# First attention, branch a: scores stacked over 128 rows instead of 64, with their operands split into roundings and remainders

## The chip, the core and the metric

The kernel is one program on one core of a Trainium2 chip. The metric is device time in microseconds (us); three runs of the kernel before gave 1660.15, 1660.17 and 1661.46 us, with a median of 1660.17 us.

The core's engines are named as in the profile: PE is TensorE (PEld its weight loads), DVE is VectorE, ACT is ScalarE, POOL is GpSimd, SP is SyncE, which here only issues transfers. All matrix products write to PSUM, eight banks of 128x512 fp32.

## What is computed

Two blocks run one after the other over 512 tokens of width 1024. Only the first attention of the first block is touched. In the reference it reads (shortened):

```python
def first_block(x, norm_gain, w_in, b_merge, rel_bias, ...):
    xn = rms_norm(x, norm_gain[0])
    qa, ka, va, ga, qb, kb, vb, gb, iq, ik, iw, za, zb = jnp.split(xn @ w_in[0], offsets, axis=-1)
    ya = chunked_relpos_attention(qa, ka, va, rel_bias[0]) * jax.nn.silu(ga)   # branch a, 8 heads of 64
    ...
    yb = dsa_sparse_attention(qb, kb, vb, iq, ik, iw) * jax.nn.silu(gb)        # branch b
    ...

def one_chunk(c):                                # inside chunked_relpos_attention
    s = jnp.einsum('bqhd,bkhd->bhqk', qc, kc).astype(jnp.float32) * scale + bias[None]
    s = jnp.where(valid[None, None], s, NEG)
    p = jax.nn.softmax(s, axis=-1).astype(v.dtype)
    return jnp.einsum('bhqk,bkhd->bqhd', p, vc)
```

All of it has to have fp32 accuracy.

## The kernel before

**Weights as slabs.** All weights come from DRAM as a stream of slabs of 128x1024 fp32 (512 KB) into RAW, a ring of four. For each slab `n`, ACT writes a rounded copy to WH (`high`, L1360, type fp32r) and POOL writes the remainder RAW - WH to WL (`low`, L671). A product in fp32 accuracy is then three fp32r products: WH with the rounded and with the remaining part of the input (L782, L783), and WL with the rounded part (L784). WH and WL hold two slabs, so ACT may round slab n only when slab n-2 has been used up, and POOL's remainder must be there before PE starts on slab n. Most jobs (`qa0`, `ga2` and so on) have one slab each and one PSUM bank, which ACT or DVE empties. In the order of the stream the jobs here are vbiw, iq0, iq1, ikb, qa0 to qa3, ka0 to ka3, va (four slabs), qb0 to qb3, ga0 to ga3, gb0 to gb3, za0 to za7. PE works through them in that order, with the indexer's products between qa1 and va.

**Queues.** Each engine runs its instructions in the order in which they are written; it waits at a semaphore (`wait_ge`) with all that stands behind it. Transfers are issued by SP (the slabs) and, in between its own work, by ACT. `split_past(name)` on ACT does the roundings of all slabs up to two behind the job's last one; `evac` calls it, waits for the job's products and empties its bank.

**The first attention** (`attention(segments["ab"])` on PE, ACT and DVE) goes over 32 pairs: first branch a, then branch b, each with four head pairs p and in each four blocks i of 128 queries. One pair is two heads e = 0, 1 against P * (i + 1) keys. In step k PE makes the scores of pair k (L919), two k-tiles of the jobs za and zb beside them (L782 to L784), the value products of pairs k-4 and k-3 (L894, in every second step) and the transposes of the probabilities of pair k-2 (L941). DVE adds the bias and takes the maximum (L2048) and later normalises (L2026, L2030); ACT takes the exponentials (L1455) and copies the transposed tile (L1466).

In branch a a head's scores are one product of 64 rows in full fp32: heads e = 0 and 1 lie in the lower and the upper 64 partitions of QA and KA. In branch b they are two fp32r products over 128 rows:

```python
yield dict(qk=[(QA[r, p, P * i:P * i + P], KA[r, p, 0:w])], w=w,           # steps_a
...
q = QS[:, h, P * i:P * i + P]                                              # steps_b
...
yield dict(qk=[(q, KBH[:, 0:w]), (q, KBL[:, 0:w])], w=w,
```

QS holds per head the rounded query in one half of the partitions and its remainder in the other; KBH and KBL hold the rounded keys and their remainders in both halves. `query_high` (ACT, L1558) and the line after it on DVE (L2177) fill QS for branch b.

**Around it.** DVE makes the index of branch b (`selection`, L2151, L2152) from 88 us on, and between its parts scales the banks of ga, gb (`first_scaled`, L1935), for which ACT waits (`xscaled`) before it empties them, and turns the queries of branch b (`rope`, L1955 to L1957). The turned halves come over four transfers QB to QBT (L1548), for which POOL has cleared QBT at the very start (L696).

## Time and profile before

| | us |
|---|---|
| median of three runs | 1660.17 |
| profiled execution | 1663.26 |
| its span in the profile | 1661.5 |
| PE busy in the span | 1648.2 (99%) |
| DVE, ACT, POOL busy | 927.3, 796.9, 714.3 |
| branch a in the span | about 175 to 227 |
| branch b in the span | about 227 to 286 |

The span is the time from the first to the last instruction in the profile; the profiled execution lasts 1.8 us longer. The profile page gives the busy time of each engine, a row of slices over the span, the DMA queues, the chain of work that ended last and the costliest groups of instructions. The trace behind it gives every instruction with its start; there, "idle before" is the time in which an engine waited, and the arrow names the instruction that released it. PE's granted clock was 1.00 of full speed in all stretches between 30 and 330 us.

### The profile page before, as it was taken

To read this page: it belongs to the slowest core of one execution; us is meant where nothing else is said; L and a number is where in the kernel's file an instruction comes from. 1 tells how busy PE (TensorE), PEld (TensorE's weight loads), DVE (VectorE), ACT (ScalarE), POOL (GpSimd) and SP (SyncE) were. 2 spreads that over 40 slices of the span, in tenths; PEclk is the share of its full clock that TensorE was granted. 3 is DMA by queue.
4 is the path that set the end of the run, shared out by engine and by line. 5 is a ranking of instruction groups with operands and counts; after the bars stand their busy time and mean duration, and the time that the engine had idled before them with its cause. 6 is when DMAs were issued, how large, how long until landed. Compare 5 with 4: busy or idle time off the path is not lost.

```text
span 1661.5 us, 24530 instructions
## 1 busy us (share of the span) xinstructions
PE 1648.2 (99%) x8381; PEld 1364.3 (82%) x8381; DVE 927.3 (56%) x1746; ACT 796.9 (48%) x1239; POOL 714.3 (43%) x378
## 2 busy tenths in 40 slices
PE   9999999999999999999999999999999999999999
PEld 6788678888988899888888888888888888888887
DVE  6799877559447488646555531153673555555100
ACT  6334566336464545445454433336775544544222
POOL 4344212444644576344444444544312444444445
PEclk9999999999999999999999999999899999999999
DMA  6233211433423210223332333333102232332333
GB/s 225 77 114 108 77 39 51 166 101 103 130 88 100 77 39 27 64 89 102 91 99 92 98 101 112 103 95 102 39 26 64 89 101 89 100 98 91 103 113 114
DMA packets 44381, 153.56 MB, mean 92 GB/s; under 512 B 4976, under 2 KB 5104, under 8 KB 44272
## 3 DMA queue, kind: packets, MB, share of 16 engines
q1 hardware_dynamic: 41184, 145.10, 27.5%
q10 hardware_dynamic: 3120, 7.43, 1.4%
q8 instruction: 49, 0.80, 0.2%
q14 instruction: 28, 0.23, 0.0%
HBM read 150.15 MB, written 2.10 MB: 92 GB/s over the span
## 4 chain that ended last, share of the span: by engine, by line
PE 90%; DVE 5%; issue 2%; ACT 1%; POOL 1%; DMA 0%; POOLq 0%; SPq 0%; ACTq 0%; DVEq 0%
PE DB L782 9%; PE DB L1231 9%; PE DB L1233 9%; PE DB L1232 9%; PE DB L784 9%; PE DB L783 9%; PE DB L1250 5%; PE DB L1251 5%; PE DB L1252 5%; PE SC L919 3%; PE DB L941 2%; PE SC L1113 2%; PE DB L837 2%; PE DB L839 1%; PE DB L838 1%
## 5 line engine op out<-in xcount | busy, mean ns | idle before, releaser
L671 POOL TENSOR_TENSOR WL<-RAW,WH 128x1024 fp32r<-128x1024 f32 x257 | 620.0, 2413 | 889.6 <-ACT WH L1360 886.9
L1360 ACT ACTIVATE WH<-RAW 128x1024 fp32r<-128x1024 f32 x257 | 272.4, 1060 | 573.4 <-PE DB L1252 174.3
L1231 PE MATMUL DB<-XH,WH 128*128 128x512 f32 x640 | 249.0, 389 | 0.0
L1232 PE MATMUL DB<-XL,WH 128*128 128x512 f32 x640 | 249.0, 389 | 0.0
L1233 PE MATMUL DB<-XH,WL 128*128 128x512 f32 x640 | 249.0, 389 | 0.0
L782 PE MATMUL DB<-XH,WH 128*128 128x512 f32 x568 | 228.6, 403 | 0.9 <-POOL WL L671 0.4
L784 PE MATMUL DB<-XH,WL 128*128 128x512 f32 x568 | 221.8, 390 | 0.0
L783 PE MATMUL DB<-XL,WH 128*128 128x512 f32 x568 | 221.4, 390 | 0.0
L1233 PEld LDWEIGHTS DB<-XH,WL 128*128 128x128 f32 x640 | 120.2, 188 | 25.0
L1232 PEld LDWEIGHTS DB<-XL,WH 128*128 128x128 f32 x640 | 120.2, 188 | 25.0
L1231 PEld LDWEIGHTS DB<-XH,WH 128*128 128x128 f32 x640 | 120.2, 188 | 24.7
L1251 PE MATMUL DB<-GL,WH 128*128 128x512 f32 x352 | 137.0, 389 | 0.0
L1250 PE MATMUL DB<-GH,WH 128*128 128x512 f32 x352 | 137.0, 389 | 0.0
L1252 PE MATMUL DB<-GH,WL 128*128 128x512 f32 x352 | 136.9, 389 | 0.0
L782 PEld LDWEIGHTS DB<-XH,WH 128*128 128x128 f32 x568 | 106.8, 188 | 30.8 <-issue 7.6
L784 PEld LDWEIGHTS DB<-XH,WL 128*128 128x128 f32 x568 | 106.6, 188 | 22.9
L783 PEld LDWEIGHTS DB<-XL,WH 128*128 128x128 f32 x568 | 106.9, 188 | 19.7 <-issue 0.2
L2465 DVE TENSOR_TENSOR DB<-DB,SQ 128x512 f32<-128x512 f32 x88 | 61.2, 696 | 42.6 <-PE DB L1233 41.9
L1252 PEld LDWEIGHTS DB<-GH,WL 128*128 128x128 f32 x352 | 66.1, 188 | 13.8
L1250 PEld LDWEIGHTS DB<-GH,WH 128*128 128x128 f32 x352 | 66.1, 188 | 13.7
L1251 PEld LDWEIGHTS DB<-GL,WH 128*128 128x128 f32 x352 | 66.1, 188 | 13.7
L2470 DVE SCALAR_TENSOR_TENSOR SB<-DB,CW,SB 128x511 f32<-128x511 f32 x44 | 33.0, 750 | 73.9 <-ACT SB L1773 73.9
(539 smaller groups left out, 3012.7 us busy)
## 6 DMA issues: line engine op xcount, KB each, us to landing
RAW<-in_stream_dram SPq DMA_DIRECT2D x267, 512.0 KB, 3.5
TP<-in_toep_dram ACTq DMA_DIRECT2D x4, 512.0 KB, 3.6
X<-in_xt_dram ACTq DMA_DIRECT2D x1, 2048.0 KB, 14.1
out_dram<-X SPq DMA_DIRECT2D x8, 256.0 KB, 4.5
X<-in_xt_dram ACTq DMA_DIRECT2D x4, 256.0 KB, 6.3
X<-in_xt_dram SPq DMA_DIRECT2D x4, 256.0 KB, 6.1
MRAW<-in_memt_dram ACTq DMA_DIRECT2D x2, 512.0 KB, 4.6
CONST<-in_consts_dram SPq DMA_DIRECT2D x1, 448.0 KB, 8.8
```

The lines of the kernel that those rows point to most:

```text
L671: nc.gpsimd.tensor_tensor(WL[:, s, :], RAW[:, j, :], WH[:, s, :].bitcast(F32), ALU.subtract).then_inc(lo_done, 1)
L782: mm(o, WH[:, s, c], hi(k), start=(k == 0), stop=False)
L783: mm(o, WH[:, s, c], lo(k), start=False, stop=False)
L784: last = mm(o, WL[:, s, c], hi(k), start=False, stop=(k == job.kts - 1))
L1231: mm(o, WH[:, s, c], xh(k), start=(k == 0), stop=False)
L1232: mm(o, WH[:, s, c], xl(k), start=False, stop=False)
L1233: last = mm(o, WL[:, s, c], xh(k), start=False, stop=(k == KD - 1))
L1250: mm(o, WH[:, s, c], GH[:, k, :], start=(k == 0), stop=False)
L1251: mm(o, WH[:, s, c], GL[:, k, :], start=False, stop=False)
L1252: last = mm(o, WL[:, s, c], GH[:, k, :], start=False, stop=(k == FF - 1))
L1360: A(WH[:, n % SPLIT, :], RAW[:, n % RING, :], ACT.Copy).then_inc(hi_done, 1)
L2465: V.tensor_tensor(DB[j], DB[j], SQ[:, 0, :], ALU.mult).then_inc(scaled, 1)
```

## The change

The scores of branch a take the form of branch b. `steps_a` now takes its queries from QS and its keys from two new stacks, KAS (rounded) and KAL (remainders), each with eight tiles of 128x512.

- *Queries.* ACT rounds the four tiles of QA into the even tiles of QS (`first_query_high`, four times 128x512) between the slab roundings of va. POOL writes the remainders over QA (QAL, `query_rest`), one after each of four slab remainders. Three transfers of 64 partitions x 4 tiles (512 KB) bring the halves to their places: one is issued after slab va3's rounding, two after qb0 is emptied.
- *Keys.* ACT rounds two tiles of KA into KAS after qb2 is emptied and two after ga0 is emptied (`first_key_high`); KAS lies over QA and KA, hence the order 0, 2, 1, 3. POOL writes the remainders to KAL (`key_rest`): two after the remainder of slab ga0, one after that of ga1, one after that of ga2. Four transfers are issued after ga2 and ga3, two more after gb0. PE waits for the last of them ahead of the first scores.
- *Moved.* QS is now in use for branch a, so `query_high(p)` and DVE's remainder of branch b's queries move into the attention: behind the last pair of head pair p. QBT moves to the place of PT and SQ, its clearing on POOL to behind the query remainders, and `rope` comes one `first_scaled` earlier, since KAL takes QBT's old place.

```diff
--- before.py
+++ after.py
@@ -210,6 +210,7 @@
 CROSSED = {(0, 1): 0, (1, 2): 1, (2, 3): 2, (0, 2): 3, (1, 3): 4, (0, 3): 5}
+KEY_ORDER = [0, 2, 1, 3]
 YLSLOT = [0, 6, 2, 3, 4, 5]
...
@@ -283,8 +284,11 @@
         ZA = at("ZA", [P, KD, TOK], A0 + 71)
-        QBT = at("QBT", [P, 4, TOK], A0 + 71)
+        QBT = at("QBT", [P, 4, TOK], 100)
         QS = at("QS", [P, NHEAD, TOK], 0, F32R)
+        QAL = at("QAL", [P, 4, TOK], A0 + 0, F32R)
+        KAS = at("KAS", [P, NHEAD, TOK], A0 + 0, F32R)
+        KAL = at("KAL", [P, NHEAD, TOK], A0 + 71, F32R)
         KBH = at("KBH", [P, TOK], A0 + 56, F32R)
...
@@ -388,6 +392,12 @@
             return MRAW[k // 4][:, k % 4, :]
+
+        def key_high(p, e):
+            return KAS[:, 2 * KEY_ORDER.index(p) + e, :]
+
+        def key_low(p, e):
+            return KAL[:, 2 * p + e, :]
 
...
@@ -446,6 +456,13 @@
         qs_low = sem("qs_low")
+        qa_high = sem("qa_high")
+        qa_low = sem("qa_low")
+        qa_in = sem("qa_in")
+        ka_high = sem("ka_high")
+        ka_in = sem("ka_in")
+        ka_low = sem("ka_low")
+        ka_moved = sem("ka_moved")
         x_again = sem("x_again")
...
@@ -547,7 +564,8 @@
                         h = 2 * p + e
-                        yield dict(qk=[(QA[r, p, P * i:P * i + P], KA[r, p, 0:w])], w=w,
+                        q = QS[:, h, P * i:P * i + P]
+                        yield dict(qk=[(q, key_high(p, e)[:, 0:w]), (q, key_low(p, e)[:, 0:w])], w=w,
                                    bias=TP[:, p % 2, e, TOK - w:TOK],
...
@@ -674,6 +692,10 @@
                 a, b = -(-first // RING), end // RING
+                if b <= a:
+                    for n in range(first, end):
+                        low(n % RING, n)
+                    return
                 for n in range(first, a * RING):
...
@@ -693,10 +715,35 @@
             s0 = JOBS["hg0"].slabs[0]
-            nc.gpsimd.memset(QBT[:, :, :], 0.0).then_inc(turn_clear, 1)
             low(0, 0)
             low_in_halves(1)
-            lows(2, JOBS["za7"].done + SPLIT)
+            def query_rest(p):
+                pool.wait_ge(qa_high, p + 1)
+                nc.gpsimd.tensor_tensor(QAL[:, p, :], QA[:, p, :], QS[:, 2 * p, :].bitcast(F32),
+                                        ALU.subtract).then_inc(qa_low, 1)
+
+            def key_rest(p):
+                pool.wait_ge(ka_high, KEY_ORDER.index(p) + 1)
+                nc.gpsimd.tensor_tensor(key_low(p, 0), KA[:, p, :], key_high(p, 0).bitcast(F32),
+                                        ALU.subtract).then_inc(ka_low, 1)
+
+            n = JOBS["va"].slabs[0] + 1
+            lows(2, n)
+            for p in range(4):
+                low((n + p) % RING, n + p)
+                query_rest(p)
+            pool.wait_ge(vb_turned, 1)
+            pool.wait_ge(roped, 4)
+            nc.gpsimd.memset(QBT[:, :, :], 0.0).then_inc(turn_clear, 1)
+            m = JOBS["ga0"].slabs[0] + 1
+            lows(n + 4, m)
+            for p in KEY_ORDER[:2]:
+                key_rest(p)
+            for p in KEY_ORDER[2:]:
+                low(m % RING, m)
+                m += 1
+                key_rest(p)
+            lows(m, JOBS["za7"].done + SPLIT)
             lows(JOBS["za7"].done + SPLIT, HALVED[1])
...
@@ -905,6 +952,9 @@
                             pe.wait_ge(*wait)
+                        if pair[0]["kind"] == "a" and k == 0:
+                            pe.wait_ge(qa_in, 48)
+                            pe.wait_ge(ka_in, 32)
                         if pair[0]["kind"] == "b" and pair[0]["first"]:
...
@@ -1530,9 +1580,32 @@
             A(KBH[:, :], KBT[:, :], ACT.Copy).then_inc(kb_high, 1)
+            def first_query_high(p):
+                act.wait_ge(dve_emptied, EMPTIED[JOBS[f"qa{p}"].banks[0]][1])
+                A(QS[:, 2 * p, :], QA[:, p, :], ACT.Copy).then_inc(qa_high, 1)
+
+            def first_key_high(p):
+                act.wait_ge(dve_emptied, EMPTIED[JOBS[f"ka{p}"].banks[0]][1])
+                A(key_high(p, 0), KA[:, p, :], ACT.Copy).then_inc(ka_high, 1)
+
+            def rows_to(out, src, done):
+                act.dma_start(out.bitcast(F32), src.bitcast(F32)).then_inc(done, 16)
+
+            low_half, high_half = HALF
+            even, odd = slice(0, NHEAD, 2), slice(1, NHEAD, 2)
+
+            act.wait_ge(xl_done, KD)
+            first_query_high(0)
+            first_query_high(1)
             while split_next[0] < JOBS["va"].done + SPLIT - 1:
...
                 split_next[0] += 1
+                if split_next[0] == JOBS["va"].done - 1:
+                    first_query_high(2)
+                    first_query_high(3)
+                elif split_next[0] == JOBS["va"].done:
+                    act.wait_ge(qa_high, 4)
+                    rows_to(QS[high_half, odd, :], QS[high_half, even, :], qa_in)
             for t in range(NT):
...
@@ -1541,6 +1614,15 @@
                 evac(f"qb{k}", QB[:, k, :], scale=DH ** -0.5)
+                if k == 0:
+                    act.wait_ge(qa_low, 4)
+                    act.wait_ge(qa_in, 16)
+                    rows_to(QS[low_half, odd, :], QAL[high_half, :, :], qa_in)
+                    rows_to(QS[high_half, even, :], QAL[low_half, :, :], qa_in)
+                if k == 2:
+                    act.wait_ge(qa_in, 48)
+                    for p in KEY_ORDER[:2]:
+                        first_key_high(p)
             act.wait_ge(turn_clear, 1)
...
@@ -1559,17 +1641,28 @@
                 scaled_evac(f"ga{k}", GA[:, k, :], ACT.Silu)
-                if k == 3:
-                    query_high(0)
+                if k == 0:
+                    act.wait_ge(ka_low, 2)
+                    for p in KEY_ORDER[2:]:
+                        first_key_high(p)
+                if k >= 2:
+                    keys = (KAS, KAL)[k - 2]
+                    act.wait_ge(ka_low, 4)
+                    rows_to(keys[high_half, odd, :], keys[high_half, even, :], ka_moved)
+                    rows_to(keys[low_half, odd, :], keys[high_half, even, :], ka_moved)
             for k in range(4):
                 scaled_evac(f"gb{k}", GB[:, k, :], ACT.Silu)
-                if k < 3:
-                    query_high(k + 1)
+                if k == 0:
+                    act.wait_ge(ka_moved, 64)
+                    for keys in (KAS, KAL):
+                        rows_to(keys[high_half, even, :], keys[low_half, even, :], ka_in)
             def next_bias(s):
...
                     scaled_evac(f"za{done}", ZA[:, done, :], ACT.Identity, bias=col("bm0", done))
+                if s["kind"] == "a" and s["last"]:
+                    query_high(s["grp"])
                 if s["kind"] == "a" and s["last"] and s["grp"] < 2:
...
@@ -2159,8 +2252,8 @@
                 first_scaled(SCALED[k])
-                if 2 <= k < 6:
-                    rope(2 + k, QB[:, k - 2, :], COSB[:, :], SINB[:, :], QBT[:, k - 2, :], (qb_turned, 16 * 4))
+                if 1 <= k < 5:
+                    rope(3 + k, QB[:, k - 1, :], COSB[:, :], SINB[:, :], QBT[:, k - 1, :], (qb_turned, 16 * 4))
                 for _ in range(3 if k < 2 else KD if k == 6 else 0):
...
@@ -2171,10 +2264,11 @@
                     V.tensor_tensor(KBL[:, :], KBT[:, :], KBH[:, :].bitcast(F32), ALU.subtract).then_inc(kb_low, 1)
-                if 1 <= k <= NHEAD:
-                    p, e = divmod(k - 1, 2)
-                    dve.wait_ge(qs_high, k)
-                    V.tensor_tensor(QS[HALF[1 - e], k - 1, :], QB[HALF[e], p, :], QS[HALF[e], k - 1, :].bitcast(F32),
+                p, e = k // 4 - 1, k % 4 - 1
+                if 0 <= p < 4 and 0 <= e < 2:
+                    h = 2 * p + e
+                    dve.wait_ge(qs_high, h + 1)
+                    V.tensor_tensor(QS[HALF[1 - e], h, :], QB[HALF[e], p, :], QS[HALF[e], h, :].bitcast(F32),
                                     ALU.subtract).then_inc(qs_low, 1)
...
```

## Rows read from the trace of the kernel before

**Rows 1.** Part 1 of the page: busy time, share of the span.

```profile
PE 1648.2 (99%) x8381; PEld 1364.3 (82%) x8381; DVE 927.3 (56%) x1746; ACT 796.9 (48%) x1239; POOL 714.3 (43%) x378
```

**Rows 2.** Chain of waits: start us, us, what; four repeats.

```profile
205.01 0.87 PE DB L941 x8
...
219.29 0.87 PE DB L941 x8
...
246.13 0.87 PE DB L941 x8
...
259.23 0.87 PE DB L941 x8
```

**Rows 3.** PE timeline, branch a, 256 columns: start, us, line, operation.

```profile
216.20 0.87 PE L941 MATMUL DB<-CONST,PB 128*128 128x128 f32 x6
217.00 0.70 PE L919 MATMUL SC<-KA,QA 64*128 64x256 f32 x4
...
217.97 0.39 PE L783 MATMUL TB<-XL,WH 128*128 128x512 f32 x1
```

**Rows 4.** PE timeline, branch b, 256 columns.

```profile
256.48 0.88 PE L941 MATMUL DB<-CONST,PB 128*128 128x128 f32 x6
257.12 0.48 PE L919 MATMUL SC<-KBH,QS 128*128 128x256 f32 x2
...
257.90 0.39 PE L783 MATMUL DB<-XL,WH 128*128 128x512 f32 x1
```

**Rows 5.** ACT timeline around the slab ga0; idle time before in brackets.

```profile
133.08 3.21 ACTq L1548 DMA_DIRECT2D QBT<-QB  x4
136.89 1.06 ACT L1360 ACTIVATE WH<-RAW 128x1024 fp32r<-128x1024 f32 x1 [3.90 <-PE DB L784]
137.97 1.28 ACT L1381 ACT_TABLE_LOAD   x1
139.26 0.60 ACT L1381 ACTIVATE GA<-DB 128x512 f32<-128x512 f32 x1
142.33 1.06 ACT L1360 ACTIVATE WH<-RAW 128x1024 fp32r<-128x1024 f32 x1 [2.46 <-PE DB L784]
```

**Rows 6.** POOL timeline, the remainder of slab ga2.

```profile
138.03 2.40 POOL L671 TENSOR_TENSOR WL<-RAW,WH 128x1024 fp32r<-128x1024 f32 x1 [3.04 <-ACT WH L1360]
```

**Rows 7.** PE timeline, first product on slab ga2.

```profile
142.13 0.39 PE L782 MATMUL DB<-XH,WH 128*128 128x512 f32 x1
```

**Rows 8.** POOL by line and shape: busy, mean ns, idle before.

```profile
L689 POOL TENSOR_TENSOR WL<-RAW,WH 128x512 fp32r<-128x512 f32 x10 | 13.1, 1310 | 25.7 <-ACT WH L1357 25.7
...
L738 POOL TENSOR_TENSOR KRL<-KRD,KRH 128x512 fp32r<-128x512 f32 x6 | 8.7, 1462 | 9.8 <-ACT KRH L1861 9.6
...
L696 POOL MEMSET QBT<- 128x2048 f32 x1 | 1.8, 1805 | 0.3 <-POOLq L2771 0.3
```

**Rows 9.** ACT by line from 87 to 176 us: busy, mean ns, idle before.

```profile
L1360 ACT ACTIVATE WH<-RAW 128x1024 fp32r<-128x1024 f32 x17 | 18.1, 1062 | 56.4 <-PE DB L784 43.8 <-PE DB L839 12.6
L1558 ACT ACTIVATE QS<-QB 64x512 fp32r<-64x512 f32 x8 | 5.0, 622 | 0.1
...
L1532 ACT ACTIVATE KBH<-KBT 128x512 fp32r<-128x512 f32 x1 | 0.6, 613 | 0.0
```

**Rows 10.** DMA issues, part 6 of the page: KB each, us to landing.

```profile
RAW<-in_stream_dram SPq DMA_DIRECT2D x267, 512.0 KB, 3.5
...
X<-in_xt_dram ACTq DMA_DIRECT2D x1, 2048.0 KB, 14.1
```

**Rows 11.** ACT timeline in branch b, the copy after a pair's last exponentials.

```profile
244.30 0.82 ACT L1466 ACTIVATE PT<-DB 128x768 f32<-128x768 f32 x1 [1.47 <-PE DB L941]
```

**Rows 12.** Busy time of all engines, four pairs of branch b.

```profile
247.00:260.10 13.10, 13.10 (x102) 10.89 (x101) 10.14 (x36) 8.68 (x22) 2.39 (x1) 1.00 0.13 42
```

**Rows 13.** DVE timeline, the two products of a rotation.

```profile
148.65 0.68 DVE L1955 TENSOR_TENSOR TMP<-QBT,SINB 128x512 f32<-128x512 f32 x1
149.37 2.78 DVE L1956 TENSOR_TENSOR QB<-QB,COSB 128x512 f32<-128x512 f32 x1
```

## The prediction

> **What bounds the kernel now.** I read the busy times first, then the chain of waits, then the timeline of each engine around the first attention. TensorE is busy for 1648.2 of 1661.5 us, the next engine for 927.3 [rows 1]. The chain of waits runs through TensorE's own instructions over the whole stretch that is changed: the same eight transposes come back every 14.28 us in branch a (219.29 - 205.01) and every 13.10 us in branch b (259.23 - 246.13), and nothing but TensorE's work stands between them [rows 2]. So an edit counts in two cases only: it changes TensorE's own work, or it delays something until TensorE has to wait for it. Everything that ScalarE (ACT), VectorE (DVE), GpSimd (POOL) and the queues gain or lose short of that is worth nothing.
>
> How late may the others be? A weight slab takes 5.44 us of products (ACT starts a slab's rounding when the slab before the last is used up: 136.89, then 142.33 [rows 5]). Rounding (1.06), handover and remainder (2.40) of slab ga2 end at 138.03 + 2.40 = 140.43 [rows 5, 6], and its first product is at 142.13 [rows 7]. The reader is to see one number in this: 1.7 us of slack per slab, for ACT and POOL together.
>
> **Step 1, the scores on TensorE: -4.7 us.** Removed are 32 score products of 64 rows with full fp32 operands (64 instructions on KA, QA); added are 64 products over 128 rows, two per head. Branch b's scores have this very form now, and its pairs are otherwise the same (two weight tiles beside each pair, the same transposes and value products). At 256 columns, from the start of the transposes ahead to the second weight product behind, branch a takes 217.97 - 216.20 = 1.77 us [rows 3] and branch b 257.90 - 256.48 = 1.42 us [rows 4]: 0.35 less. Over the four widths of one head pair it is the difference of the periods, 14.28 - 13.10 = 1.18 us [rows 2]; four head pairs give 4 x 1.18 = 4.7 us. The bounds are close, since the form is measured: 4.4 to 4.9, as the first scores stand behind weight products and not behind transposes.
>
> The Trainium skill, TensorEngine Tiling (Array Packing), Key Properties, says that row tiles work in parallel, and FP8 and Floating Point Precision, TensorE Precision Notes, that true fp32 takes four passes. By both, two heads of four passes side by side would stream as many columns as four single products, and this step would be worth nothing. The trace disagrees: 1.77 against 1.42 us. The same section of the tiling page says that a change of tiling mode drains TensorE, which would put the loss of the old form ahead of and behind the scores; no run here separates that yet.
>
> **Step 2, more work on ACT: hidden.** Eight roundings of 128x512 at 0.61 us [rows 9] are 4.9 us in all. Over 17 slabs ACT was idle for 56.4 us ahead of the slab roundings, 3.3 us each [rows 9], and at most two new ones (1.2 us) fall into one gap. Nine transfers are issued: four issues to QBT took 3.21 us, 0.8 each [rows 5], so two take 1.6 us. Both together are 2.8 of 3.3 us, and beyond that lies the slack of 1.7. Without this cover the issue of one pair of transfers would cost up to 1.1 us.
>
> **Step 3, more work on POOL: hidden, but for one place.** Eight remainders of 128x512 cost 1.31 to 1.46 us [rows 8] and the clearing of QBT, now in the stream of slabs and no longer ahead of it, 1.8 us [rows 8]. POOL is idle for 3.04 us between slabs [rows 6]. One remainder per slab fits. After slab qb0 come a remainder and the clearing, 1.4 + 1.8 = 3.2 us: 0.2 late, under the slack. After ga0 come two remainders, 2.8 us: fits. At the start nothing is won; POOL waits there for the first rounding anyway.
>
> **Step 4, the wait that is new: +2.05 us.** POOL's order is: remainder of slab ga1, key remainder of head pair 1, remainder of slab ga2, key remainder of pair 3. The key remainder waits for ACT's key rounding, and ACT makes that only after it has emptied the bank of ga0. Queued behind POOL's wait is the remainder of slab ga2, for which TensorE waits. In numbers: ACT rounds slab ga2 at 136.89, loads a table at 137.97, empties ga0 at 139.26 for 0.60 [rows 5], rounds the keys until about 139.8 + 0.61 = 140.4; POOL's key remainder lasts 1.31 and ends at 141.7 (141.9 with 1.46); slab ga2's remainder then takes 2.40 [rows 6] and ends at 144.15 to 144.3. It ended at 140.43 before, so the delay is 3.7 to 3.9 us, of which 1.7 are slack. TensorE starts the slab at about 144.2 and not at 142.13 [rows 7]: 2.05 us, bounds 1.8 to 2.4. The next slabs are in time: ga3's remainder ends near 147.9, and TensorE wants it 5.44 us after 144.2.
>
> **Step 5, the transfers: hidden.** Each moves 512 KB from 64 partitions. The trace shows no landing of such a transfer. A slab of 512 KB lands in 3.5 us, four times as much in 14.1 us [rows 10]; I take 3.5 to 7 us each, nearer the first, which has the size. Two go out at about 117 us and are awaited at 127.5; four are out by 158 and are awaited near 162, with two more behind them that TensorE awaits at 175. The loads of slabs run three slabs ahead and do not notice.
>
> **Step 6, what moves into the attention: hidden.** Per head pair ACT gets two roundings of 64x512, 2 x 0.62 us [rows 9], right after the pair's last exponentials, ahead of a copy before which it now waits 1.47 us for TensorE in the faster form [rows 11]: 0.2 left. DVE gets its eight remainders at other steps, two in a period of 13.10 us of which it is busy for 10.14 [rows 12]. Neither reaches TensorE. Without that cover the roundings would cost 4 x 1.24 = 5 us.
>
> **The sum.** -4.7 + 2.05 = -2.7 us. It is made against the profiled execution, a span of 1661.5 us in a run of 1663.26, which would become 1658.8. The median of the runs is 1660.17, so the forecast is 1657.5 us, 0.16% less.
>
> **The rivals.** *First, POOL's wait is covered:* were the key rounding early enough (say, ahead of the table load and the bank), or a later stall of TensorE shortened by it, only step 1 is left: 1660.17 - 4.7 = 1655.4. Against it stands the order of the two queues, which is fixed.
>
> *Second, DVE falls behind.* Its second product of a rotation took 2.78 us where the first took 0.68 [rows 13]: it started at 149.37, while POOL worked on a slab remainder. In the changed kernel the first rotation comes one slab earlier, at about 143.5, when POOL has three operations without a gap (step 4). DVE could be up to 4 us late with ga2, ACT waits for it before it empties the bank and issues transfers, and slab roundings slip by 1 to 3 us beyond their slack. Price: 1 to 3 us more, 1659.5. It decides where DVE scales ga2 later than some 155 us. The Trainium skill, SBUF — State Buffer, Who interferes with whom, says that a DVE instruction with two SBUF inputs and a GpSimd one that reads SBUF exclude each other for a whole instruction; the trace agrees, with 2.78 us for one such product.
>
> *Third, the other side: the transfers are slow.* The place is ACT's wait for the three query transfers after qb2, at 127.5 us. Behind it stand two key roundings and two remainders (0.7 + 2 x 1.35) and then slab ga1 (2.4), which TensorE needs at 136.7. It decides from a landing at 130.9 on, 14 us after the issue; from there each us costs one. If each transfer took four times a slab's 3.5 us and they ran one after the other, 28 us, the price would be 13.8 us: about 1671. Against it stands that 2048 KB land in 14.1 us [rows 10].
>
> *Fourth, step 1 brings nothing,* as the columns alone would have it, and the stall stays: 1660.17 + 2.05 = 1662.2. Rows 3 and 4 speak against it.
>
> **Chances.** Forecast 0.60; POOL's wait covered 0.15; DVE behind 0.15; slow transfers 0.06; no gain on TensorE 0.04. A measurement of this kernel tells about 0.2% (3.3 us) from no change, so faster means below 1656.9 and slower above 1663.5. The forecast lies 0.6 us from that bound; of its 0.60 I give 0.13 to faster. Faster: 0.15 + 0.13 = 0.28. Slower: 0.06, and 0.01 of the second. Same: 0.65. The range reaches from the first rival (1655.2) to past the middle of the second (1660.5).
>
> **What the profile of the changed kernel would show.** Step 1: the eight transposes every 13.1 us in branch a. Step 4: TensorE idle for about 2 us near 142 us ahead of a first weight product, released by POOL's slab remainder, and POOL idle before its third key remainder, released by ACT. Step 2, 3: no wait of TensorE for a slab between 88 and 142. Step 5: landings under 7 us. Step 6: no wait of TensorE between 176 and 225. Second rival: DVE's scaling of ga2 after 155 us. The forecast is wrong if the idle near 142 is missing, or if a second one of over 1 us appears.

## The result and the profile after

The changed kernel takes 1663.64 us, the kernel before 1661.21 (medians of 22 runs each; ranges 1660.32 to 1665.78 and 1660.07 to 1663.29). The ratio is 1.0018, 95% interval 1.0012 to 1.0024: 3.0 us slower by the ratio, 2.4 by the medians, where 2.7 us less was forecast. Both are under the 0.2% named in the prediction, but the time lies outside its range and on the other side of no change. About 1.0 of the 6.1 us between 1657.5 and 1663.64 is the base: the prediction reckoned from a median of three runs (1660.17), and the median of 22 is 1661.21.

The profiled execution of the kernel before (1663.26 us) lies at the upper end of its runs, that of after (1663.63 us) in the middle of its own, so the two spans (1661.5 and 1661.8 us) hide most of the difference. I read the lag of the changed kernel at one point: the last eight transposes of the attention. The chain of waits has them in the kernel before at

```profile
283.90 1.06 PE DB L941 x8
```

and in the kernel after, where L941 has become L991, at

```profile
285.98 1.06 PE DB L991 x8
```

2.08 us late. Up to there all of the change has happened, and behind it nothing differs but TensorE's granted clock between 1150 and 1190 us (0.87 of full in the kernel before's execution, 0.96 and 0.86 in the two halves of after's), over which after's execution made up 1.7 us.

**The scores are faster, as forecast.** The TensorE timeline of after, branch a, from the transposes of 256 columns on; it answers to [rows 3]:

```profile
219.31 0.88 PE L991 MATMUL DB<-CONST,PB 128*128 128x128 f32 x6
219.94 0.48 PE L969 MATMUL SC<-KAS,QS 128*128 128x256 f32 x2
220.26 0.40 PE L969 MATMUL SC<-KAL,QS 128*128 128x256 f32 x2
...
220.73 0.39 PE L830 MATMUL TB<-XL,WH 128*128 128x512 f32 x1
```

220.73 - 219.31 = 1.42 us, as branch b had it [rows 4]. The chain of waits of after has branch a's eight transposes 13.10 us apart (14.28 in [rows 2]):

```profile
195.85 0.87 PE DB L991 x8
...
208.95 0.87 PE DB L991 x8
```

**TensorE waits where it did not.** The waits of TensorE in after (engine, tile and line, releaser, us in total, times, longest):

```profile
PE DB L829 <- POOL WL L689: 3.4, 4, 2.7
PE DB L829 <- ACT GA L1431: 1.9, 1, 1.9
```

The kernel before has 0.8 us over three times for the first, with 0.4 as the longest, and nothing for the second. The others are alike, but for one of 1.3 us for DVE at the very start, which costs nothing: the first slab product is at 8.90 us (8.87 before). In TensorE's timeline of after the new ones are

```profile
142.00 0.39 PE L831 MATMUL DB<-XH,WL 128*128 128x512 f32 x1
144.32 0.53 PE L829 MATMUL DB<-XH,WH 128*128 128x512 f32 x1 [1.93 <-ACT GA L1431]
144.65 0.63 PE L830 MATMUL DB<-XL,WH 128*128 128x512 f32 x1
145.08 0.63 PE L831 MATMUL DB<-XH,WL 128*128 128x512 f32 x1
...
148.04 0.39 PE L829 MATMUL DB<-XH,WH 128*128 128x512 f32 x1
...
173.01 0.39 PE L831 MATMUL DB<-XH,WL 128*128 128x512 f32 x1
176.06 0.47 PE L829 MATMUL DB<-XH,WH 128*128 128x512 f32 x1 [2.67 <-POOL WL L689]
```

The first product of slab ga2 starts at 144.32 (142.13 in [rows 7]; 0.10 of the difference was there already), a second idle of 2.67 us stands at 173.4, and behind the first idle products follow each other every 0.43 us and no longer every 0.23. The windows of after, with the columns as in [rows 12], show that it is the clock:

```profile
137.00:142.00 5.00, 5.00 (x24) 4.13 (x22) 4.80 (x10) 3.97 (x5) 1.45 (x2) 1.00 0.37 126
144.30:148.00 3.70, 3.68 (x9) 2.93 (x10) 3.63 (x3) 0.00 (x0) 3.70 (x2) 0.54 0.46 142
148.00:152.00 4.00, 4.00 (x19) 3.27 (x18) 3.90 (x7) 0.33 (x1) 0.65 (x1) 1.00 0.44 131
```

TensorE was granted 2.4 GHz up to the idle, 1.2 GHz for nearly all of the 3.7 us behind it (0.54 of full), and 2.4 again. The nine products from 144.32 to 148.04 took 3.72 us; the first nine behind the second idle, at the full clock, took 2.16 (176.06 to 178.22). So the half clock cost about 1.6 us (the expectations below reckon with 1.75).

**Why POOL is late at 142, and ACT at 168.** POOL's timeline and ACT's, in after:

```profile
140.55 1.30 POOL L727 TENSOR_TENSOR KAL<-KA,KAS 128x512 fp32r<-128x512 f32 x1 [5.46 <-ACT KAS L1589]
141.81 2.36 POOL L689 TENSOR_TENSOR WL<-RAW,WH 128x1024 fp32r<-128x1024 f32 x1
```

```profile
154.40 1.40 ACTq L1592 DMA_DIRECT2D KAS<-KAS  x2
157.11 1.06 ACT L1410 ACTIVATE WH<-RAW 128x1024 fp32r<-128x1024 f32 x1 [2.12 <-PE DB L831]
157.86 0.60 ACTq L1592 DMA_DIRECT2D KAL<-KAL  x1
...
158.50 2.37 ACTq L1592 DMA_DIRECT2D KAL<-KAL  x1
162.55 1.06 ACT L1410 ACTIVATE WH<-RAW 128x1024 fp32r<-128x1024 f32 x1 [3.90 <-PE DB L831]
163.52 0.58 ACT L1431 ACTIVATE GB<-DB 128x512 f32<-128x512 f32 x1
171.06 0.60 ACTq L1592 DMA_DIRECT2D KAS<-KAS  x1
171.69 0.63 ACTq L1592 DMA_DIRECT2D KAL<-KAL  x1
172.43 1.06 ACT L1410 ACTIVATE WH<-RAW 128x1024 fp32r<-128x1024 f32 x1 [8.33 <-issue]
```

POOL: 5.46 us idle for ACT's key rounding, with the remainder of slab ga2 queued behind, which ends at 144.17. (The releaser named for the first idle, ACT's emptying of a bank, is not the cause: in the runs below that emptying stays, and the idle goes with POOL's order alone.) ACT: after gb0 is emptied, at 163.52, it waits for the first four transfers until 171.06. The last of them was issued at 158.50 and took 12.5 us, 16.6 us from the first of the four issues. Behind that wait stands the rounding of the next slab, due at 162.55 + 5.44 = 167.99 and made at 172.43: 4.4 us late, of which 1.7 are slack, 2.7 idle. The page's DMA issues have these transfers with their median landings:

```profile
KAS<-KAS ACTq DMA_DIRECT2D x3, 512.0 KB, 4.8
KAL<-KAL ACTq DMA_DIRECT2D x3, 512.0 KB, 9.7
```

and the window of the wait shows a DMA share of 0.92 (the last number but one; the one before it is the granted clock):

```profile
160.00:173.40 13.40, 13.39 (x60) 10.75 (x58) 7.36 (x7) 2.51 (x4) 3.08 (x2) 1.00 0.92 225
```

The account of this execution at 286 us: -4.68 (scores) + 2.09 (the first idle, with what is left of smaller waits) + 1.56 (half clock) + 2.67 (second idle) + 0.44 (not assigned) = +2.08.

### The profile page after: what moved, and what is told of

Its sections match the earlier page's. It is cut to its first block, busy times and chain, and to the rows that moved or that the text cites. A ratio compares the mean times of both kernels' runs of the same rounds, so it can differ in the third digit from the quotient of the medians.

```text
span 1661.8 us, 24544 instructions
## 1 busy us (share of the span) xinstructions
PE 1642.7 (99%) x8381; PEld 1368.5 (82%) x8381; DVE 927.5 (56%) x1746; ACT 801.1 (48%) x1247; POOL 724.3 (44%) x386
## 3 DMA queue, kind: packets, MB, share of 16 engines
q1 hardware_dynamic: 41184, 145.10, 28.0%
q10 hardware_dynamic: 5568, 12.15, 2.7%
## 4 chain that ended last, share of the span: by engine, by line
PE 89%; DVE 4%; issue 3%; POOL 2%; ACT 2%; DMA 0%; POOLq 0%; SPq 0%; ACTq 0%; DVEq 0%
PE DB L1282 9%; PE DB L1281 9%; PE DB L1283 9%; PE DB L829 9%; PE DB L831 8%; PE DB L830 8%; PE DB L1300 5%; PE DB L1302 5%; PE DB L1301 5%; PE SC L969 2%; PE SC L1163 2%; PE DB L991 2%; PE DB L884 1%; PE DB L885 1%; PE DB L886 1%
## 6 DMA issues: line engine op xcount, KB each, us to landing
X<-in_xt_dram ACTq DMA_DIRECT2D x1, 2048.0 KB, 14.1
```

## The experiments

My theory after the result: the form gives 4.7 us, POOL's order costs the first idle, the late issue and slow landing of the key transfers the second, and each idle costs more than its length through the clock. The rivals: the second idle is only a consequence of the first; the moved work has a cost of its own; the lower clock is a chance of the one execution.

**The form alone.** The kernel before, branch a's scores as two products over all 128 rows. They read XH and XL, so nothing has to be prepared for them, and branch a's output is not the reference's:

```diff
-    yield dict(qk=[(QA[r, p, P * i:P * i + P], KA[r, p, 0:w])], w=w,
+    q = XH[:, h, P * i:P * i + P]
+    yield dict(qk=[(q, XH[:, p, 0:w]), (q, XL[:, p, 0:w])], w=w,
```

> The kernel before, with branch a's scores as two products of 128 rows each, read from XH and XL where they lie; nothing is rounded, subtracted or moved for them, so branch a's output is not the reference's. The form of the scores alone. Ledger theory (the form gives 4.7 us and the rest of the change costs 7): 4.7 us faster than before, ratio 0.9972, and in the trace the same eight transposes come back every 13.1 us in branch a, with no new wait of TensorE. Rival (the columns alone count, the form is worth nothing and the change loses its time elsewhere): within 0.5 us of before, a period of 14.3 us.

1658.22 us, ratio 0.9981 (0.9972 to 0.9990): 3.0 us less, where 4.7 were expected. The period is 13.1, but TensorE's waits are longer than in the kernel before, where the first of these lines read 1.2, 2 and the second 0.9, 2:

```profile
PE SC L920 <- DVE ST L2049: 1.6, 3, 1.0
...
PE DB L942 <- DVE PB L2031: 1.5, 3, 0.7
```

In the faster form DVE, which makes branch b's query remainders in the first pairs, comes too late. So part of the 4.7 needs the move of that work.

**The form with step 6.** The same, with `query_high(p)` and DVE's remainders behind the last pair of each head pair, as the change has them:

```diff
-                if k == 3:
-                    query_high(0)
...
+                if s["kind"] == "a" and s["last"]:
+                    query_high(s["grp"])
```

> The kernel before with the form of the scores alone (XH and XL as operands, branch a's output is not the reference's), and branch b's query roundings on ACT and remainders on DVE moved into the attention as the change moves them. The first run of the form alone won 3.0 us by the runs and had 1 us of new waits for DVE between 176 and 204 us. Theory (those waits came from DVE's eight remainders at the head of branch a, which the faster pace no longer hides, and the change moves them away): they go, and the kernel is 4.4 to 4.9 us faster than before. Rival (the roundings on ACT now stand in the way, 0.2 us over their cover): waits of TensorE for ACT behind each head pair's last pair, and no more than 3 us won.

1656.92 us, ratio 0.9974 (0.9964 to 0.9984): 4.4 us less by the medians, and the waits are those of the kernel before. The form and step 6 belong together; together they are worth nearly what step 1 of the prediction said (4.7, bounds 4.4 to 4.9).

**Everything but the form.** The changed kernel, with branch a's scores on 64 rows again, read from QB, so that branch a's output is not the reference's:

```diff
-    q = QS[:, h, P * i:P * i + P]
-    yield dict(qk=[(q, key_high(p, e)[:, 0:w]), (q, key_low(p, e)[:, 0:w])], w=w,
+    yield dict(qk=[(QB[r, p, P * i:P * i + P], QB[r, p, 0:w])], w=w,
```

> The changed kernel with all its roundings, remainders and transfers, but branch a's scores in the old form, 64 rows and full fp32, read from QB (branch b's queries) as queries and keys; branch a's output is not the reference's. The moves without the form. Ledger theory (form -4.7, moves +7): 4.7 us slower than the changed kernel, about 1668, 7 us slower than before, with the period of the transposes at 14.3 us and the two idles of TensorE near 142 and 173 us as in the changed kernel. Rival (the moves also slow the attention itself): more than 8 us slower than before, with new waits between 180 and 235 us.

1668.9 us (four runs, 1666.46 to 1671.26), ratio 1.0044 (1.0029 to 1.0060): 7.6 us more. With -4.4 for the form that makes +3.2, against +2.4 measured for the whole, within what four runs tell. Preparing the operands costs some 7 us, and the only new waits of TensorE are the two of the changed kernel (3.2 and 1.9 us), none of them inside the attention.

**POOL's order.** The changed kernel, with both slab remainders ahead of the key remainders that wait for ACT:

```diff
-            for p in KEY_ORDER[2:]:
+            for _ in KEY_ORDER[2:]:
                 low(m % RING, m)
                 m += 1
+            for p in KEY_ORDER[2:]:
                 key_rest(p)
```

> The changed kernel with one change of order on POOL: the remainders of slabs ga1 and ga2 first, then the key remainders of head pairs 1 and 3. Ledger theory: the idle of TensorE near 142 us (2.1 us) goes, and with it the 3.7 us at half the granted clock behind it (1.75 us); the wait near 173 us stays at about 2.7 us. 2 to 3.9 us faster than the changed kernel, about 0.5 us from before on either side. Rival (TensorE's lower clock comes from the heavier traffic of transfers and not from the idle): only 2.1 us are won, and the lower clock shows up near 144 us all the same.

1663.68 us, ratio 1.0017 (1.0008 to 1.0025). The first idle is gone, and the time is the same: I had expected 2 to 3.9 us less. TensorE's timeline and windows show where they went:

```profile
174.51 0.77 PE L830 MATMUL DB<-XH,WH 128*128 128x512 f32 x1 [4.66 <-POOL WL L689]
175.07 0.63 PE L831 MATMUL DB<-XL,WH 128*128 128x512 f32 x1
```

```profile
168.00:173.00 5.00, 1.85 (x9) 1.19 (x7) 3.01 (x7) 2.11 (x3) 0.98 (x1) 1.00 0.64 149
175.00:180.00 5.00, 5.00 (x13) 3.86 (x12) 0.00 (x0) 0.00 (x0) 1.87 (x1) 0.50 0.73 239
```

The second idle grew from 2.67 to 4.66 us, now with half the clock behind it (0.50). TensorE came to it 3.55 us earlier (the last product ahead of it is at 169.46, in the changed kernel at 173.01), but ACT's wait for the four transfers ended only 1.55 us earlier (169.51 against 171.06); the other 2.0 us became idle, and some 3 us were lost at the half clock behind it. That the second idle only follows from the first is refuted; and ACT's timeline in this run shows a second thing about the transfers:

```profile
155.74 3.50 ACTq L1593 DMA_DIRECT2D KAL<-KAL  x2
...
170.89 1.06 ACT L1411 ACTIVATE WH<-RAW 128x1024 fp32r<-128x1024 f32 x1 [9.81 <-issue]
```

Two issues that take 0.6 to 0.7 us each elsewhere held ACT for 3.5 us. A third thing stands just ahead of them:

```profile
153.09 0.60 ACT L1432 ACTIVATE GA<-DB 128x512 f32<-128x512 f32 x1 [4.24 <-DVE DB L2029]
153.09 1.37 ACTq L1593 DMA_DIRECT2D KAS<-KAS  x2
```

ACT waited 4.24 us for DVE before it could empty ga2 and issue the KAS pair, so that this pair went out only 2.65 us ahead of the KAL pair. In the changed kernel the same wait is 1.65 us (the pair at 154.40). DVE's lateness thus helped to crowd the four transfers together; how much that cost is not shown, as no run has DVE in time.

**The wait one step later.** The changed kernel, with the last two transfers and the wait ahead of them after gb1 (`if k == 1:` for `if k == 0:`):

> The changed kernel with the last two transfers of the keys, and the wait of ACT for the four ahead of them, after gb1 and not after gb0. Ledger theory: ACT no longer holds back the rounding of slab gb3, the idle near 173 us (2.7 us) goes, and the kernel is 2.7 us faster than the changed one, 0.3 us from before. Rival (the last two transfers then land too late and TensorE waits for them ahead of the first scores): the idle comes back as a wait of 1 to 4 us there, and nothing is won.

1663.09 us, ratio 1.0009 (1.0000 to 1.0019), with a wide spread, 1659.35 to 1667.2. The rival came: the idle for the slab is gone, and the first scores wait instead:

```profile
179.81 0.41 PE L969 MATMUL SC<-KAS,QS 128*128 128x128 f32 x2 [2.55 <-DMA KAL<-KAL]
```

So the chain is late as a whole: four transfers, then two that wait for them. It can't be cured at its end.

**The issue earlier.** The changed kernel, the four key transfers after ga1 and ga2 and no longer after ga2 and ga3, once without and once with POOL's new order:

```diff
-                if k >= 2:
-                    keys = (KAS, KAL)[k - 2]
+                if 1 <= k < 3:
+                    keys = (KAS, KAL)[k - 1]
```

> The changed kernel with the four transfers of the keys after ga1 and ga2 and not after ga2 and ga3, and POOL's order left as in the change. Ledger theory: the idle near 173 us goes, the one near 142 us (2.1 us) stays with its part at the lower clock: 2 to 4 us slower than the version with both edits (1656.8), so 1659 to 1661. Rival (ACT's wait for the key remainders, now after ga1, makes a third wait): an idle of TensorE near 148 us.

1659.37 us, ratio 0.9991 (0.9982 to 1.0000). The second idle is gone; the first stays at 1.9 us, with a granted clock of 0.67 from 145 to 150 us.

> The changed kernel with POOL's new order, and the four transfers of the keys issued one slab earlier, after ga1 and ga2. Ledger theory: both waits and the slow stretch go, what is left is the form: 4.7 us faster than before, 1656.5, ratio 0.9972. Rival (the new work on ACT, POOL and DVE costs in itself, beyond the two waits): 1 to 3 us slower than that, with waits of TensorE in places that the changed kernel doesn't show.

1656.81 us (1655.66 to 1657.79), ratio 0.9974 (0.9964 to 0.9984). No new wait is left, and the time is that of the form alone (1656.92). This kernel beats both: 4.4 us less than before and 6.8 less than the change. ACT's timeline in it:

```profile
143.63 1.37 ACTq L1593 DMA_DIRECT2D KAS<-KAS  x2
...
153.07 0.60 ACT L1432 ACTIVATE GA<-DB 128x512 f32<-128x512 f32 x1 [4.24 <-DVE DB L2029]
153.08 1.27 ACTq L1593 DMA_DIRECT2D KAL<-KAL  x2
154.45 1.06 ACT L1411 ACTIVATE WH<-RAW 128x1024 fp32r<-128x1024 f32 x1 [0.77 <-issue]
...
160.80 0.60 ACTq L1593 DMA_DIRECT2D KAS<-KAS  x1
161.44 0.63 ACTq L1593 DMA_DIRECT2D KAL<-KAL  x1
```

Issued as pairs nearly 10 us apart, none is held up, and the last two go out at 160.8 where they went at 171.06.

**The pairs apart, but late.** POOL's new order, the KAS pair after ga1 and the KAL pair after ga3 (`if k in (1, 3):` with `keys = (KAS, KAL)[k // 2]`), to tell "too late" from "too many at once":

> The changed kernel with POOL's new order, the two transfers of KAS after ga1 and the two of KAL after ga3, where the changed kernel has them. Against the version with the new order alone (1663.7 us, the transfers to KAL issued at 155.7, the last landed at 169.5) only the KAS pair is moved. Backlog theory (the KAL pair lands late since the KAS pair and the slabs fill the DMA engines ahead of it, and the issue itself is held up): the KAL pair, issued at the same time, lands within 8 us, its second issue takes under 1 us, ACT's wait after gb0 ends before 164.5, no idle of TensorE near 170; 4.4 us faster than before, 1656.9. Rival (the KAL pair is late because of where it is issued): it lands near 169 us again, and the kernel takes 1662 to 1664 us.

1657.46 us, ratio 0.9977 (0.9968 to 0.9987). The KAL pair was issued at 155.86, as in the run with POOL's order alone (155.74), and held ACT for 1.27 us and not for 3.50; the longest landing was 8.7 us and not 12.6. So it is the number in flight far more than the moment. The lateness is left as a small wait (1.4 us the longest, where the kernel before has 0.4) and 0.6 us; ACT's wait ended at 164.72, a little later than I had said:

```profile
155.86 1.27 ACTq L1593 DMA_DIRECT2D KAL<-KAL  x2
...
164.72 0.60 ACTq L1593 DMA_DIRECT2D KAS<-KAS  x1
165.35 2.07 ACTq L1593 DMA_DIRECT2D KAL<-KAL  x1
```

The last line is a long issue with a single transfer of ACT's in flight ahead of it, beside a slab.

**The transfers by themselves.** The kernel before, with copies of XH of the same shape (64 partitions, 512 KB) on ACT's queue, one after ga0, two after ga2, four after gb0:

```diff
+                if k == 2:
+                    copies([(SPARE, half) for half in HALF])
...
+                if k == 0:
+                    copies([(tile, half) for tile in (SPARE, SPARE2) for half in HALF])
```

> The kernel before, with transfers of the changed kernel's shape and size (64 partitions, four tiles of 128x512 in every second place, 512 KB, SBUF to SBUF) from XH to unused tiles: one after ga0, two together after ga2, four together after gb0. Nobody waits for them but the next group. Theory (the transfers are bound by the DMA engines, some 2.4 us each at the full rate and in line with the slabs): the single one lands in 4 to 5 us, the last of two in 6 to 7.5, the last of four in 11 to 13.5. Rival (each has a fixed time of its own, and the long ones of the changed kernel had another cause): all land in 4 to 6 us.

This was run once (1661.54 us). One landed in 4.9 us, of two the later in 6.6, of four the last in 12.0, each counted from its own issue. The issue of the last three of the four held ACT:

```profile
159.57 0.60 ACTq L1568 DMA_DIRECT2D SPARE<-XH  x1
...
160.20 5.27 ACTq L1568 DMA_DIRECT2D SPARE<-XH  x3
...
166.83 1.06 ACT L1363 ACTIVATE WH<-RAW 128x1024 fp32r<-128x1024 f32 x1
```

That is 1.76 us each where 0.6 is usual, the longest 2.57. Counted from its own issue, the last landing grows by some 2.4 us for each further transfer, (12.0 - 4.9) / 3. Whoever waits for the whole group waits from the first issue: 7.3 us for the two (148.94 to 156.22) and 15.4 for the four (159.57 to 174.93), with the slabs in between. The page's DMA queues give the same from another side: ACT's queue moved 12.15 MB in after and 7.43 before, and took 2.7% and 1.4% of 16 engines' span. 4.72 MB in 1.3% of 1662 us are 218 GB/s, 2.4 us for 512 KB with all engines; the slabs' queue moved 145.10 MB in 27.5% (kernel before), 317 GB/s, 1.65 us. The percentages are rounded, so the first is good to some 20 GB/s. The packets differ too: the nine transfers are 2448 packets of 1.9 KB on average, the slabs 41184 of 3.5 KB, so whether the 64 partitions or the smaller packets make the difference is not shown.

**The price of an idle.** The kernel before, with POOL clearing a spare tile ahead of slab ga2's remainder, 2048 + 2048 elements wide and 2048 + 1024:

```diff
+            pool.wait_ge(hi_done, m + 1)
+            nc.gpsimd.memset(SPARE[:, 0:2048], 0.0).then_inc(spare, 1)
+            pool.wait_ge(spare, 1)
+            nc.gpsimd.memset(SPARE[:, 0:2048], 0.0).then_inc(spare, 1)
```

> The kernel before with one delay and nothing else: ahead of the remainder of slab ga2, once that slab is rounded, POOL clears 128x2048 of unused SBUF twice (3.65 us). TensorE's wait is 3.65 - 1.7 = 1.9 us by the slack. Theory (an idle of TensorE of about 2 us costs more than itself, since the granted clock falls to half behind it in a part of the executions): 2 to 4.5 us slower than before, by the median 3 or so, and a wider spread than before has. Rival (the clock fell in the changed kernel for another reason, such as the transfers): 1.9 us slower, with the spread of before.

> The same delay with 128x2048 and 128x1024 cleared (2.75 us): TensorE's wait is about 1.0 us. Theory: 1 us if an idle of that length leaves the granted clock alone, up to 3.5 if it doesn't. Rival (slack other than 1.7 us): the wait in the trace differs from 1.0 by more than 0.3, and so does that of the longer delay.

The wider one makes an idle of 2.0 us and costs 2.7 us by the medians (1664.03, ratio 1.0020, 1.0011 to 1.0029), but 1.2 in its quickest run and 5.9 in its slowest. Its profiled execution, the quickest, kept a clock of 1.00:

```profile
144.37 0.47 PE L791 MATMUL DB<-XH,WH 128*128 128x512 f32 x1 [1.98 <-ACT GA L1390]
```

Over the whole kernel the mean granted clock was 0.999 in its five quickest runs and 0.995 in the slowest. The narrower one makes 1.2 us and costs 0.7 (1661.96, ratio 1.0007, 0.9998 to 1.0016), with a spread of 1.9. So an idle of 2 us costs its length, and in some executions more, which their lower mean clock fits (the one trace of this kernel is of a quick execution); one of 1.2 us showed nothing beyond its length, though its interval reaches to 2.7 us. That is a test of the price, made in the kernel before and at the same place as the change's first idle.

## Why the prediction was wrong

**The sum as it should have been,** by the medians of the runs: the form, with step 6, -4.4; the first idle +2.6 (1659.37 - 1656.81, early issue without and with POOL's order); the second +4.3 (1663.64 - 1659.37, late issue and early); together +2.5, measured +2.4. Forecast were -4.7 + 2.05 + 0.

The two idles can't be priced apart, though. With the late issue, POOL's order is worth nothing (1663.64 and 1663.68), with the early one 2.6 (1659.37 and 1656.81); and the early issue is worth 4.3 with the old order and 6.9 with the new. While the transfers were late, they set the time, whatever was won ahead of them. What is firm is the form with step 6 (-4.4) and both idles together (+6.8).

- **Step 1 was right:** 1.42 us as in branch b, a period of 13.10, 4.4 us in the time. By the two statements of the Trainium skill that the prediction sets against it (TensorEngine Tiling (Array Packing), Key Properties, and FP8 and Floating Point Precision, TensorE Precision Notes) it would have been worth nothing; the runs show otherwise. Whether the rest of that rule explains it, the change of tiling mode, stays open: no run separated it.
- **Steps 2, 3 and 6 were right** in that none made a wait of TensorE. Step 2 priced an issue at 0.8 us; the fourth of the keys took 2.37, and ACT still waited 3.90 us for TensorE behind it. Step 6 is more than hidden: without it 1.3 us of step 1 are lost (1658.22 against 1656.92). I had costed it only as work that needs cover, and not as the removal of work from a place where DVE was about to be late.
- **Step 4 was right in its mechanism and its moment,** 144.2 forecast and 144.32 found; its size was short. The idle lasted the 2.05 us forecast (2.09), but the term for the clock behind it was missing: 1.6 us in the profiled execution, and 2.6 for both by the medians of the pair with the early issue. [Rows 7] and its surroundings could not show it, as the kernel before has no such idle there.
- **Step 5 failed, and with it the sign.** "Four are out by 158 and are awaited near 162" was written down and not worked out. The bound of 3.5 to 7 us was that of one transfer; four beside a stream of slabs took up to 12.5. The slabs' loads, which were not to notice, slowed as well, from 3.5 us to 8.5 and 10.0, but came in time. Even by my own bound for a single one, four at 3.5 to 7 us sharing 16 engines could not land in 4 us: [rows 10] has 2048 KB, the size of four, at 14.1 us, and I read that row only as a bound for the query side. The four issued from 155 to 158 would have landed between 169.1 and 172.1 and the next slab's rounding, behind two issues of 0.65, have come at 170.4 to 173.4, where it could be no later than 168.0 (as measured in after) + 1.7 = 169.7: a term of 0.7 to 3.7 us. The runs have 2.7 us of idle in the profile and 4.3 by the medians (1663.64 against 1659.37). The prediction's own signs for this step, a landing over 7 us and a second idle of over 1 us, both came. The Trainium skill, DMA: Bandwidth & Descriptors, Queues, rings and completion order, says that the queues of SP and ACT are rings on the same 16 engines; the trace agrees: from 150 to 175 us of after the queue of ACT's transfers took 50.4% and that of the slabs 26.3% of the time of the 16 engines.
- **The third rival had the right kind of event at the wrong place.** It put slow transfers at ACT's wait after qb2, where a landing up to 14 us after the issue would do, and gave them 6 in 100; in after they landed by 122.4, 6.5 us after the issue. The wait after gb0, 4 us behind the last issue, had no deadline worked out.
- **The second rival's event came, without the price named there.** DVE scaled ga2 at 153.66 in after, near the 155 us that I had named, as its rotation took from 143.57 to 149.20, 5.6 us, beside three operations of POOL. In the fastest kernel ACT waits 4.24 us for just that, and TensorE waits for nothing. But in the changed kernel it put off the first pair of key transfers by 1.65 us, toward the second, and may have had a share in the price of step 5; no run separates it.
- **The other two** are out: nothing shortened the first idle, and the form is worth 4.4. (The first rival's 1660.17 - 4.7 is 1655.5; the range's lower end of 1655.2 is not that number.)

## What to carry to other kernels

For each wait that a change adds, work out the deadline behind it (what is queued there, and when it is due) and the landing with all that is in flight, not that of one transfer: here that is, from the first issue to the last landing, 4.9 us for one, 7.3 for two and 15.4 for four. Issue transfers in small groups as soon as their source is ready; a change of order alone was worth 6.8 us, more than the whole idea of the change. And reckon with the granted clock behind an idle of TensorE of about 2 us and more: the price is the idle and, in some executions, half the clock for some us. Last, price waits together: here removing the first idle alone was worth nothing as long as the second stood.

## What the runs showed of the hardware

- **TensorE's clock after an idle.** 1.2 GHz for nearly all of 3.7 us after 1.9 us of idle (changed kernel; the same with the early issue alone), over all of 175 to 180 us after 4.66 us, and again from 175 to 180 us after 3.2 us (everything but the form). But after 1.9 us in that last run and in the one with the wait a step later, after 2.0 us in the profiled execution of the wide clearing and after 2.67 us in the changed kernel the clock stayed at 1.00. What decides between them stays open. Some kernels with such an idle spread more widely (5.5 us over the changed kernel's runs, 4.7 with the wide clearing), others don't (1.9 with the idle of 4.66). Each run's mean granted clock goes roughly with its time: 1.000 in the changed kernel's quickest run, 0.996 or 0.997 in the eight of 1665 us and more. Where in those runs it fell is not recorded.
- **A busy queue holds the issuing engine.** An issue of 512 KB on ACT took 0.6 to 0.7 us, with two or three before it in flight up to 2.57, and once 2.07 with only one and a slab.
- **Transfers between 64-partition halves of SBUF** used the engines for half as long again as slabs from memory: 218 and 317 GB/s at full share, with packets of 1.9 and 3.5 KB on average. Which of the two makes the difference is open.
- **DVE beside POOL.** In after the three operations of a rotation took 1.15, 1.65 and 2.76 us beside POOL's remainders, where one alone takes 0.68 [rows 13].
